# Key pages of the sparse-attention indexer scored four ring items at a time instead of two, in a two-layer decoder step on one core

## What is computed

```python
def indexer_scores(qi, wi, ki):
    dots = jnp.einsum('bqhd,bkd->bqhk', qi, ki).astype(jnp.float32)
    return jnp.einsum('bqh,bqhk->bqk', wi.astype(jnp.float32), jax.nn.relu(dots)) * (D_IDX ** -0.5)
...
def dsa_sample(q, k_new, v_new, qi, wi, ki_new, pool_kv, pool_ki, layer, page_table):
    ki_past = pool_ki[layer, page_table].reshape(b, past, D_IDX)
    sc = indexer_scores(qi, wi, ki_all)
    _, idx = lax.top_k(sc, n_sel)
    return sparse_attend(q, kvg[:, :, :, 0], kvg[:, :, :, 1], valid)
```

## Time and profile before

| what | us |
|---|---|
| device time, three runs | 652.36, 655.52, 656.72 (median 655.52) |
| span of the profiled execution | 654.0 |
| TensorE busy (share of the span) | 609.3 (93%) |
| VectorE, POOL, ScalarE busy | 353.3, 267.8, 175.6 |
| bytes moved, mean rate | 198.38 MB, 303 GB/s |
| chain that ended last | TensorE 71%, DMA 14%, VectorE 5%, ScalarE 4% |

### The profile page before, as it was taken

The page is one execution under the profiler, slowest core; times in us unless marked ns, Lnnn a source line. Parts: engine busy times, 40 slices in busy tenths (PEclk is TensorE's granted clock), DMA queues, the critical chain, the costliest instruction groups (busy, mean ns, idle before and its releaser), DMA issues.

```text
span 654.0 us, 13776 instructions
## 1 busy us (share of the span) xinstructions
PE 609.3 (93%) x4870; PEld 426.8 (65%) x4870; DVE 353.3 (54%) x1058; ACT 175.6 (27%) x433; POOL 267.8 (41%) x460
## 2 busy tenths in 40 slices
PE   5999999999998978999999999899999898799993
PEld 3766555767775755667777665577677766466772
DVE  3774645766766626334257565566566844433403
ACT  3025332322214112351111352222322231126201
POOL 0507541655435675342000474146452667641000
PEclk9999999988997988999999999999889899889998
DMA  8879999999958799987967799999996978995061
GB/s 302 304 277 342 369 370 402 402 381 325 340 152 296 235 379 361 299 280 258 399 223 252 258 369 368 388 399 367 358 329 220 302 245 302 370 358 186 28 269 72
DMA packets 71606, 198.38 MB, mean 303 GB/s; under 512 B 11537, under 2 KB 40370, under 8 KB 67442
## 3 DMA queue, kind: packets, MB, share of 16 engines
q1 hardware_dynamic: 49682, 99.99, 44.0%
q0 software_dynamic: 21856, 97.50, 41.6%
HBM read 189.30 MB, written 52.00 MB: 369 GB/s over the span
## 4 chain that ended last, share of the span: by engine, by line
PE 71%; DMA 14%; DVE 5%; ACT 4%; SPq 3%; issue 2%; ACTq 0%; DVEq 0%; POOLq 0%; POOL 0%
PE bank L881 68%; DMA kv<-in_kk 8%; DMA kv<-in_vv 5%; PE bank L926 3%; SPq L415 2%; DVE st L2041 1%; ACT srow L822 1%; ACT shared L716 1%; DVE shared L1682 1%; ACT shared L733 1%; DVE st L1688 1%; DVE srow L2035 1%; DMA x<-in_x 1%; DVE xn L2117 0%; SPq L411 0%
## 5 line engine op out<-in xcount | busy, mean ns | idle before, releaser
L881 PE MATMUL bank<-xn,w 128*128 128x288 f32 x1120 | 299.9, 423 | 0.0
L881 PEld LDWEIGHTS bank<-xn,w 128*128 128x128 f32 x1120 | 212.0, 195 | 71.8 <-issue 15.2
L415 POOL DMA_DIRECT2D kv<-in_vv x160 | 86.3, 540 | 64.6 <-PE bank L881 35.3
L415 POOL DMA_DIRECT2D kv<-in_kk x128 | 69.0, 539 | 104.3 <-issue 54.7
L669 ACT ACTIVATE pt<-bank 128x288 f32<-128x288 f32 x48 | 19.7, 410 | 218.2 <-PE bank L881 218.2
L881 PE MATMUL bank<-pt,w 128*128 128x288 f32 x256 | 64.9, 407 | 0.0
L881 PEld LDWEIGHTS bank<-pt,w 128*128 128x128 f32 x256 | 48.3, 190 | 13.6 <-issue 0.8
L508 POOL DMA_DIRECT2D out_keep<-in_buf x48 | 25.3, 531 | 66.7 <-PE bank L881 66.7
L881 PE MATMUL bank<-kv,pt 128*32 128x256 f32 x512 | 39.4, 421 | 12.8 <-DMA kv<-in_vv 12.0
L1559 DVE TENSOR_SCALAR_CACHE_REDUCE hit<-sc,tb 128x516 bf16<-128x516 f32 x62 | 46.5, 750 | 2.2
L881 PE MATMUL bank<-kv,qz 128*32 128x256 f32 x512 | 34.3, 385 | 0.0
(11 more groups left out here) (246 smaller groups left out, 810.7 us busy)
## 6 DMA issues: line engine op xcount, KB each, us to landing
w<-in_w SPq DMA_DIRECT2D x86, 512.0 KB, 8.4
out_keep<-in_buf POOLq DMA_DIRECT2D x16, 2044.0 KB, 14.6
kv<-in_kk SPq DMA_DIRECT2D x128, 160.0 KB, 8.5
kv<-in_kk POOLq DMA_DIRECT2D x128, 160.0 KB, 5.8
kv<-in_vv POOLq DMA_DIRECT2D x160, 128.0 KB, 5.3
kv<-in_dil SPq DMA_DIRECT2D x24, 576.0 KB, 7.2
kv<-in_vv SPq DMA_DIRECT2D x96, 128.0 KB, 4.9
out_keep<-in_buf POOLq DMA_DIRECT2D x16, 508.0 KB, 7.6
```

The costliest lines, as they stand in the source:

```text
L415: engine.dma_start(kv[:, s, r * rec:(r + 1) * rec], a["kk" if what == "page" else "vv"][bass.ds(page + layer * N_POOL, 1)].rearrange("o p ...
L881: return pe.matmul(out, lhsT, rhs, start=start, stop=stop, skip_group_check=True, **k)
```

## The change

Key pages are taken in batches of four ring items. `page_quad(v)` replaces `page_pair(u)`: it waits for items 4v to 4v+3, and each of its products streams all four, so that an index dot has 256 columns instead of 128 and a score product 512 instead of 256. The batch gives its four ring places back together. The stage is 8 times batch, `pdots(v)`, `proj(8 + v)`; `segs(0)` stands after batch 4. ScalarE's and VectorE's programs are not touched; in SP's and POOL's only the values waited for change.

```diff
--- before.py
+++ after.py
@@ -64,6 +64,7 @@
 ROPED = [QI, QI + 1, QI + 2, QI + 3, KI, QA, QA + 1, KA, KA + 1, QC, QC + 1, QC + 2, KC, KC + 1, KC + 2]
 LATE_ROOT = 3
 NPAIR = 16
+NQUAD = 8
 NGRP = 2 * NPG
 SEQ_ORDER = (0, 2, 4, 6, 1, 3, 5, 7)
 BITS = 31
@@ -106,10 +107,11 @@
 
     used, landed, total, n = [], [], [0] * NKV, 0
     for at, (kind, i) in enumerate(RING):
-        end = f"ks{i // 8}" if kind == "page" and i // 2 % 4 == 3 else {("window", NB - 1): "dk", ("window", 2 * NB - 1): "do",
+        end = f"ks{i // 8}" if kind == "page" and i % 8 >= 4 else {("window", NB - 1): "dk", ("window", 2 * NB - 1): "do",
                                                                            ("value", NGRP - 1): "so"}.get((kind, i))
-        n += 0 if end else i % 2 if kind == "page" else 1
-        used.append((end, None) if end else ("kv_used", n + 1 - i % 2 if kind == "page" else n))
+        last = i % 4 == 3 if kind == "page" else True
+        n += 0 if end else last
+        used.append((end, None) if end else ("kv_used", n if last else n + 1))
         total[at % NKV] += 16 if kind == "window" else 64
         landed.append(total[at % NKV])
     return used, landed, total, n
@@ -156,16 +158,13 @@
     proj(7)
     use("newdots", 6)
     use("segs", 6)
-    for u in range(NPAIR):
-        c, g, p = chunk_of(u)
-        if u % 4 == 0:
-            use(f"ks{c}", (2, 5)[c % 2])
+    for v in range(NQUAD):
+        if v % 2 == 0:
+            use(f"ks{v // 2}", (2, 5)[v // 2 % 2])
             for h in range(2):
-                use(f"dots{c}{h}", 3 + h)
-        if u % 2 == 0:
-            use(f"pdots{u // 8}{u // 2 % 4}", 7)
-        else:
-            proj(8 + u // 2)
+                use(f"dots{v // 2}{h}", 3 + h)
+        use(f"pdots{v // 4}{v % 4}", 7)
+        proj(8 + v)
     use("newsegs", 7)
     for n in range(NCOUNT):
         use(f"count{n}", 4)
@@ -925,34 +924,29 @@
                 def turn(out, in_, n):
                     return pe.transpose(out, in_, ident(n))
 
-                def page_pair(u):
-
-                    c, g, p = chunk_of(u)
-                    for n in (2 * u, 2 * u + 1):
+                def page_quad(v):
+
+                    c, g = v // 2, v % 2
+                    for n in range(4 * v, 4 * v + 4):
                         pe.wait_ge(S[f"kv_in{n % NKV}"], landed(L, n))
-                    s = 2 * u % NKV
-                    if u % 4 == 0:
+                    s = 4 * v % NKV
+                    if g == 0:
                         for use in (f"dots{c}0", f"dots{c}1", f"ks{c}"):
                             pe.wait_ge(drained(use), before(L, use))
                     for r in range(4):
                         for h in range(2):
-                            use = f"dots{c}{h}"
-                            o = g * 256 + p * P
-                            ins = mm(bank_of(use)[32 * r:32 * r + 32, o:o + P].rearrange("p (i t) -> p i t", i=2),
+                            ins = mm(bank_of(f"dots{c}{h}")[32 * r:32 * r + 32, g * 256:(g + 1) * 256].rearrange("p (i t) -> p i t", i=4),
                                      qs[half(h), SEQ_ORDER[4 * g + r], :, :].rearrange("p q h -> p (q h)"),
-                                     kv[half(h), s:s + 2, r * KREC:r * KREC + 64], start=(g == 0 and p == 0))
-                            if u % 4 == 3 and r == 3:
-                                ins.then_inc(filled(use), 1)
+                                     kv[half(h), s:s + 4, r * KREC:r * KREC + 64], start=(g == 0))
+                            if g == 1 and r == 3:
+                                ins.then_inc(filled(f"dots{c}{h}"), 1)
                     for hp in range(2):
                         for r in range(4):
                             b = SEQ_ORDER[4 * g + r]
                             o = r * KREC + 64 + hp * P
-                            ins = mm(bank_of(f"ks{c}")[32 * (b // 2):32 * (b // 2) + 32, p * 256:(p + 1) * 256].rearrange("p (i k) -> p i k", i=2),
-                                     qz[:, hp, b, :], kv[:, s:s + 2, o:o + P], start=(g == 0 and p == 0 and hp == 0))
-                    if u % 4 == 3:
-                        ins.then_inc(filled(f"ks{c}"), 1)
-                    else:
-                        ins.then_inc(S["kv_used"], 1)
+                            ins = mm(bank_of(f"ks{c}")[32 * (b // 2):32 * (b // 2) + 32, :].rearrange("p (i k) -> p i k", i=4),
+                                     qz[:, hp, b, :], kv[:, s:s + 4, o:o + P], start=(g == 0 and hp == 0))
+                    ins.then_inc(filled(f"ks{c}") if g else S["kv_used"], 1)
 
                 def segs(c0):
 
@@ -1147,14 +1141,12 @@
                 ins.then_inc(filled("newdots"), 1)
                 pe.wait_ge(S["qz_ready"], nth(L, "qz_ready", 1))
                 pe.wait_ge(drained("segs"), before(L, "segs"))
-                for u in range(NPAIR):
-                    page_pair(u)
-                    if u == 8:
+                for v in range(NQUAD):
+                    page_quad(v)
+                    if v == 4:
                         segs(0)
-                    if u % 2 == 0:
-                        pdots(u // 2)
-                    else:
-                        proj(8 + u // 2)
+                    pdots(v)
+                    proj(8 + v)
                 segs(2)
                 pe.wait_ge(drained("newdots"), nth(L, "newdots"))
                 pe.wait_ge(drained("newsegs"), before(L, "newsegs"))
```

## The result

The changed kernel takes 663.46 us (median of four runs, 661.95 to 665.90), the kernel before, on the same chip, 656.12 (652.36 to 657.16): ratio 1.0148, 95% interval 1.011 to 1.0186. A second measurement gave 1.0121 [1.0066, 1.0176]. So the change costs 1.2 to 1.5% by these two ratios; the quotient of the two medians is 1.0112, inside the first interval. Each ratio leaves out executions that lie over 1.5% above the fastest of their kernel, which are five of twelve for the kernel with only the order changed, its profiled one among them (the medians of all its executions and of all those beside it stand at 1.0078), and at most three for any other. The result is within the range on record (655 to 667) and 2.5 us over its point of 661.0. It is also beyond the 1% line (the interval begins at 1.011), where the prediction had put a chance of 0.30 against 0.67 for within it.

A forecast was written before the change was run, and what follows sets the result against it. The prediction took the page stage to be bound by its DMA transfers. Adding +2.8 us per layer, 5.5 for both, to 654.0 gave a span of 659.5; with 1.5 for the median, 661.0 us, range 655 to 667.

The forecast's parts named there:

- The bound: Page stage: from item 18 on it moves at the transfers' pace, 8.5 us against 7.48 of TensorE work per step.
- The products: Batches of the page stage: 2.45 us instead of 2.76, 0.31 saved each; a step then takes 7.17 us.
- The first release: Start of the page stage: SP and POOL begin to load 1.07 us later, which is not caught up.
- Item 18 and batch 4: Mid-stage, layer 1: item 18 lands late, batch 4 starts at 396.8 after a wait of some 4.6 us.
- POOL's queue: Before batch 4: item 21 is freed about 1.4 us later, leaving SP's queue the engines alone; 0.7 us taken back.
- Item 30: End of stage, layer 1: lands at 421.9; with a clock spell batch 7 is ready at 423.0, so it no longer matters.
- a wait there of over 3 us: Before batch 7: listed among the signs that would show the prediction wrong.
- The windows: POOL's first two windows start only after batch 6, sharing less with item 30: 1.5 us taken back of 2.9.
- The tail: Behind the last landing: batch, pdots(7) and tile, 7.59 us instead of 5.46, +2.13 per layer.
- The clock: Behind the wait before batch 4: one spell of 1.2 GHz per layer, 1.7 us lost.
- The sum: Page stage, layer 1: 423.0 + 7.59 = 430.6 against 427.83, +2.8 us per layer, 5.5 for both.
- theory C: Formed after four experiments: wide products reach batch 7 about 1.3 us earlier, item 30 lands unchanged, wait exceeds 2 us, clock falls.

The follow-up runs named there:

- split tile: Changed kernel, with pdots(7) and five of the eight calls of projection tile 15 before batch 7, three behind it; ratio 0.9982 to the kernel before.
- useless calls: Changed kernel, with six calls of projection tile 15 made once more than needed before batch 7; ratio 1.0089 to the kernel before.

## Why the prediction was right, and where not

**The bound: right.** The stage moves at the pace of the transfers and the matmuls saved are worth nothing before the last landing. Wide and narrow products with the same split tile give 0.9982 and 0.9999.

**The products: right.** 2.45 us for a batch, forecast and measured; the step of 7.17 as well.

**The first release: right.** SP's first issue came 3.06 us after the start of the stage in layer 1 (369.63 less 366.57) instead of 1.99: +1.07.

**Item 18 and batch 4: wrong, and this is the step that failed.** The prediction had item 18 land 34.5 us into the stage (34.16 as before, +1.07 for the start, -0.7 for POOL's queue) and TensorE stand still for 4.6 us before batch 4. It landed at 31.6 and 31.7, and batch 4 waited 1.2 us in both layers. The 0.7 was the term that was mis-sized: the landing came 3.5 us sooner than 34.16 and 1.07 add up to, not 0.7. Followed from issue to landing, the last DMA of item 18 was issued at 390.25, 2.4 us later in the stage than before, and took 8.0 us instead of 12.91. Nearly all of this lies behind the third quarter of its steps. The four DMAs of an item raise one semaphore to 64, 16 steps each; step 48 came at 29.8 us instead of 29.2, the last 16 took 1.9 us instead of 5.0. The runs also say which part of the change brings it: item 18 landed at 33.2 and 35.0 with only the order changed, at 32.7 and 33.8 with four places given back together, at 32.1 and 31.6 with the wait for four, all with narrow products. So the products have no part in it; by which of the transfers queued around it those last steps were held up before was not tested. A wait before batch 4 as the longest of its stage came in one of the four stages measured (2.28 us, with a spell of the lower clock behind it).

**Item 30: right in the landing, wrong in what waits for it.** Forecast 59.6 us after the start of the stage (421.9 less 362.27), measured 59.5 (layer 1) and 60.3 (layer 0). But since batches 4 to 6 had not been held up, batch 7 was ready at 56.5 (426.33 less 3.22) rather than at 60.7. So the wait stood before batch 7, in the place where the prediction had written that "item 30 no longer matters". Its own list named this, a wait there of over 3 us, as a sign of being wrong.

**The windows: the right mechanism, about half the size.** The relief from their later start was put at 1.5 us. Holding them back moved the landing of item 30 by 3.1 and 3.7 us in the kernel before and by 2.7 and 2.4 in the changed one, so the later start was worth about 0.9, an estimate from the two pairs. With 0.9 for 1.5 the forecast of the landing would be 60.2, also between the 59.5 and 60.3 measured, so the landing alone doesn't tell the two apart.

**The tail: right.** At full clock it is 7.59 us (useless calls, layer 1; 5.46 before), and the split that shortens it to 4.10 removes the loss.

**The clock: right in kind, short in size.** One spell of 1.7 us lost per layer was forecast. The four stages of the changed kernel lost 4.5, 1.6, 1.6 and 1.6: the tail of layer 0 was 12.11 us (118.36 less 106.25) against 7.59 at full clock. The Trainium skill ("TensorE: Matmul & The Clock Gate", "HAM oscillation — how this bites in real kernels") says that a loop which waits for transfers between bursts restarts each burst on the lower clock. The page stages agree for the waits over 3 us, three of three, and not for all of the shorter ones; elsewhere in these traces two waits of over 3 us left the clock alone (last section).

**The sum.** The prediction's own terms with the measured landing: 59.5 for the landing, 0.24 from landing to start, 7.59 for the tail and 1.7 for the clock make 69.0, and layer 1 took 68.96. The forecast was 68.3 (430.6 less 362.27) with a wrong wait in the middle of it; the number was close because landing and tail decide the end whichever wait stands before them. The four stages of the changed kernel average 69.4 us, +4.1 against the 2.8 forecast; of the missing 1.3, batch 7 gives back 0.8 (it starts at 59.9 on average, not at 60.7), the tails take 1.9 more than forecast (9.5 on average against 7.59, since the spells fell into three of the four and one was long), and 0.2 is that the stage of layer 0 was shorter before than the one that the forecast doubled.

**What theory C leaves open.** Wide products were expected to bring TensorE to batch 7 earlier, with the landing unchanged. It was ready 56.5 us into the stage against 57.2 with narrow ones (layer 1, first measurement), so by 0.7. But the landing was later as well: 59.5 to 60.3 in the three stages that have the wait there (57.4 in the fourth) against 58.1 to 59.2 in the two profiles with narrow products. The difference lies in the last 16 steps of item 30, 3.7 to 4.1 us against 1.9 to 2.7. The longer wait comes from both, and why the landing is later was not tested. Which of the single profiles gets a wait over 2 us, and where, varies; that the changed kernel has one in each of its four stages, and the version with narrow products in none (its longest is 1.88 us), was seen in two profiles each.

## What to carry to other kernels

Where a stage moves at the pace of its transfers, look at what stands behind the last landing: a coarser batch puts all of its own work there, and each wait that it lengthens can cost the lower clock on top. Give the engine something that doesn't need the data for exactly that wait; here 2.6 us of a tile and `pdots(7)`, moved ahead of the batch, were worth as much as the whole change had cost. A wait that goes because other transfers are held back must be looked for again behind the stage.

## What was not expected of the hardware

The last steps of item 30 come late. I followed the issues of all fourteen profiles to their landings; a gap here is the time from step 48 to step 64 of an item's semaphore, which its four DMAs share, so it is not strictly the lag of one of them. With windows in flight the gap was 1.3 to 5.6 us (3.9 and 4.1 in the changed kernel's two layers, 3.9 and 3.6 before). In the four stages in which the windows were held back it was 1.2 to 1.5 us. TensorE needs all four DMAs, so the gap alone (3.9 and 4.1 against 1.3 and 1.5 with the windows held) is about what the windows cost the changed kernel. But windows aren't its only cause: item 18, with no window in flight, had gaps of 4.5 and 5.0 us in the kernel before and of 0.9 and 1.9 in the changed one, which is the step that the prediction had wrong. The Trainium skill ("DMA: Bandwidth & Descriptors", "Why a DMA increments its semaphore by 16 and not by 1") says that the DMA engines finish their parts of one DMA independently and that only the full count means that all has landed; a DMA that runs beside others is then as late as its slowest part. The late last steps fit this; no run here shows the single engines.

The length of a wait alone doesn't say whether the clock falls. In the page stages it fell after waits of 1.85, 1.88, 2.17, 2.28, 2.54, 3.12, 3.22 and 3.24 us, and not after waits of 1.85, 1.87, 1.98 and 2.81; none under 1.85 lowered it there. The fence of the kernel with the split tile shows the 2.81, with its scores in 1.92 us; these windows of the kernel that waits for four items (second measurement) show the two sides at almost the same length, 1.88 us before 79.92 and 1.87 before 381.31:

```profile
81.00:82.00 1.00, 1.00 (x12) 0.22 (x4) 0.93 (x7) 0.00 (x0) 0.00 (x0) 0.50 1.12 391
...
382.00:383.00 1.00, 1.00 (x32) 0.38 (x24) 1.00 (x1) 0.46 (x1) 1.00 (x1) 1.00 1.06 367
```

Over the whole kernels, behind their first wait, the fourteen profiles have eighteen waits of over 3 us; within 2.5 us of the end of sixteen of them the clock was down. The two others stand in the value stage of layer 1, 3.02 us in the kernel that waits for four items (first measurement) and 3.38 in the one that frees four places together; its tile runs at full speed, 4.15 us against the 5.83 of the earlier trace rows:

```profile
573.88 1.07 PE L882 MATMUL bank<-kv,pt 128*32 128x256 f32 x16 [3.38 <-DMA kv<-in_vv]
574.88 4.15 PE L882 MATMUL bank<-xn,w 128*128 128x288 f32 x16
```

The spells in the page stages are 3.4 us of half clock, but for the one of 10.2 in layer 0 of the changed kernel; a spell costs up to half its length, less where a part of it falls into the wait. For a forecast of this kernel that means a chance of a spell from about 2 us of waiting on, and from 3 us on a spell as the likeliest case, not a certain one.
